# A decoder layer's row copies on two engines, homes of their own for window keys, and a compression weight loaded from ScalarE's queue

## What is computed

```python
kcmp = nsa_compress(full[:, :, 0], p['cmp_pe_k'], p['w_cmpk1'], p['w_cmpk2'])   # blocks of 64 rows -> one row
vcmp = nsa_compress(full[:, :, 1], p['cmp_pe_v'], p['w_cmpv1'], p['w_cmpv2'])   # gelu between the two weights
# o_c: attention over the compressed rows; their scores choose 16 blocks per query
# o_s: attention over the rows of the chosen blocks (k_sel, v_sel, from the cache pages)
# o_w: attention over a local window, the last 512 rows (k_win, v_win, from cache_win_kv)
o = g[..., 0:1] * o_c + g[..., 1:2] * o_s + g[..., 2:3] * o_w
```

## Time and profile before

| | us |
|---|---|
| median of 3 runs | 1168.5 |
| lowest, highest | 1167.29, 1168.63 |
| the profiled execution | 1166.26 |
| its span | 1164.6 |
| PE busy in the span | 1100.9 (95%) |
| DVE busy | 667.5 (57%) |
| ACT busy | 487.7 (42%) |
| POOL busy | 185.6 (16%) |
| DMA moved | 164.24 MB, mean 141 GB/s |

### The profile page before, as it was taken

The page is one execution under the profiler, slowest core; times in us unless marked ns, Lnnn a source line. Parts: engine busy times, 40 slices in busy tenths (PEclk is TensorE's granted clock), DMA queues, the critical chain, the costliest instruction groups (busy, mean ns, idle before and its releaser), DMA issues.

```text
span 1164.6 us, 22358 instructions
## 1 busy us (share of the span) xinstructions
PE 1100.9 (95%) x8538; PEld 1000.3 (86%) x8538; DVE 667.5 (57%) x1174; ACT 487.7 (42%) x773; POOL 185.6 (16%) x313
## 2 busy tenths in 40 slices
PE   6999999989599997999998989999999989999997
PEld 5888788778588785799988978899999989999997
DVE  4467993776476623566555576455533345666663
ACT  3200230357467523344334476463432234645541
POOL 1020023745123463000010030010000000001100
PEclk9999999999899998999999999999999999999999
DMA  6791253655538757476547435742542222232201
GB/s 203 172 247 54 83 186 116 175 137 129 135 86 262 230 145 226 144 214 198 189 112 258 130 107 169 262 137 84 171 138 80 79 99 78 73 109 73 73 1 77
DMA packets 172035, 164.24 MB, mean 141 GB/s; under 512 B 42341, under 2 KB 152962, under 8 KB 171802
## 3 DMA queue, kind: packets, MB, share of 16 engines
q1 hardware_dynamic: 161946, 134.77, 38.3%
q0 software_dynamic: 9984, 28.05, 8.2%
HBM read 154.21 MB, written 12.73 MB: 143 GB/s over the span
## 4 chain that ended last, share of the span: by engine, by line
PE 75%; SPq 7%; DVE 6%; issue 5%; ACT 4%; DMA 2%; POOL 0%; DVEq 0%; ACTq 0%
PE banks L1672 23%; PE banks L1926 15%; PE banks L1053 13%; PE banks L1319 3%; SPq L670 2%; PE banks L1623 2%; PE banks L1626 2%; SPq L690 2%; PE banks L1587 1%; PE banks L1059 1%; DVE rounded L3045 1%; PE banks L1386 1%; SPq L711 1%; SPq L721 1%; PE banks L1374 1%
## 5 line engine op out<-in xcount | busy, mean ns | idle before, releaser
L1672 PE MATMUL banks<-rounded 128*128 128x288 f32 (+1 forms) x2304 | 297.1, 289 | 3.1 <-DVE rounded L3172 2.6
L1672 PEld LDWEIGHTS banks<-rounded 128*128 128x128 f32 x2304 | 291.5, 188 | 6.7 <-DVE rounded L3172 3.3
L1926 PE MATMUL banks<-rounded 128*128 128x272 f32 x1536 | 195.1, 289 | 3.8 <-DVE rounded L3354 3.8
L1926 PEld LDWEIGHTS banks<-rounded 128*128 128x128 f32 x1536 | 194.5, 190 | 4.5 <-issue 3.1
L1053 PE MATMUL banks<-arena 128*128 128x256 f32 (+1 forms) x800 | 187.6, 394 | 0.0
L3045 DVE TENSOR_TENSOR rounded<-arena,rounded 128x2048 fp32r<-128x2048 f32 x63 | 146.1, 2319 | 71.0 <-ACT rounded L2156 70.9
L1053 PEld LDWEIGHTS banks<-arena 128*128 128x128 f32 x800 | 150.4, 190 | 31.8 <-issue 2.1
L2156 ACT ACTIVATE rounded<-arena 128x2048 fp32r<-128x2048 f32 x63 | 120.2, 1907 | 23.4 <-PE banks L1587 8.6
L3354 DVE TENSOR_TENSOR rounded<-arena,rounded 128x1088 fp32r<-128x1088 f32 x64 | 82.9, 1304 | 60.2 <-ACT rounded L2433 60.2
L2433 ACT ACTIVATE rounded<-arena 128x1088 fp32r<-128x1088 f32 x64 | 71.1, 1113 | 81.1 <-PE banks L1926 80.0
L2274 ACT ACTIVATE arena<-banks 128x256 f32<-128x256 f32 (+1 forms) x64 | 25.4, 397 | 126.5 <-PE banks L1672 126.5
(11 more groups left out here) (460 smaller groups left out, 1548.6 us busy)
## 6 DMA issues: line engine op xcount, KB each, us to landing
arena<-in_w_up SPq DMA_DIRECT2D x22, 1024.0 KB, 5.5
arena<-in_w_down SPq DMA_DIRECT2D x16, 1024.0 KB, 5.1
arena<-in_w_in SPq DMA_DIRECT2D x13, 1024.0 KB, 10.0
arena<-in_w_out SPq DMA_DIRECT2D x8, 1024.0 KB, 6.1
arena<-in_cache_mem_kv SPq DMA_DIRECT2D x16, 512.0 KB, 7.2
upper<-in_cache_nsa_kv SPq DMA_DIRECT2D x118, 64.0 KB, 2.2
upper<-in_cache_nsa_kv POOLq DMA_DIRECT2D x106, 64.0 KB, 2.4
arena<-in_cache_nsa_kv SPq DMA_DIRECT2D x90, 64.0 KB, 2.2
```

What stands on the lines that cost most here:

```text
L1672: ins = mm(bank(b, N), w[:, k], a[:, k, toks], start=(k == 0 and z == 0), stop=(k == K - 1 and z == 2))
L1926: ins = mm(bank(4 * (m % 2) + 2 * j + h, HALF), w[:, k, j * P:(j + 1) * P], h_split[:, t % 3, p, i, h * HALF:(h + 1) * HALF], start=(t % 1 ...
```

## The change

Four things are changed.

1. Window keys get four places of their own (`win_k`), in memory that is free after the prompt's attention. SP issues those of group 0 right after `prompt_attn_done`, those of group 1 between `sel_keys` and `sel_values`. `sel_keys` of group 1 runs in the order 0, 1, and kc 0 waits for `s_mm` 4, not 20. Window values of group 1 come last and wait for `sample_pv`; the memory rows wait for `s_mm` 40, where they waited for `snew_mm`.
2. Row copies of half 1, from tile 4 on, are shared: ACT copies tiles 4u and 4u + 2, DVE tiles 4u + 1 and 4u + 3, at pairs 8u and 8u + 1. A third semaphore, `relaid_2`, counts DVE's; `second_half_relaid` waits for both.
3. The four loads of `w2` move on SP from behind tile 7 to behind the first load of `w_cmpk1`.
4. `w_cmpv1` is loaded from ACT's queue: its first half behind the exps of pair 12, its second behind those of pair 16.

```diff
+        win_k = [place(512, at).rearrange("p (n d) -> p n d", n=WT)
+                 for at in (att0 + 4992, att0 + 5504, att0 + 1536, R + 25600)]
         def keys_page(b, kc):
-            return kv_pg[:, KV_AT[kc % 4], b, :, 0:P]
+            return win_k[b] if kc == 4 else kv_pg[:, KV_AT[kc], b, :, 0:P]
...
-                RELAY_AT.setdefault((1, 8 * _u + _k), []).append(4 * _u + _k)
+                RELAY_AT.setdefault((1 + _k % 2, 8 * _u + _k // 2), []).append(4 * _u + _k)
...
+        def second_half_relaid(eng, j):
+            if j < 4:
+                eng.wait_ge(sem("relaid_1"), j + 1)
+            else:
+                eng.wait_ge(sem("relaid_1"), 5 + (j - 4) // 2)
+                if j > 4:
+                    eng.wait_ge(sem("relaid_2"), (j - 3) // 2)
...
-            eng.wait_ge(sem("s_mm"), 20 if kc == 0 else KC_ORDER.index(kc) * 4 + 4)
+            eng.wait_ge(sem("s_mm"), KC_ORDER.index(kc) * 4 + 4)
...
                 if n == 3:
                     sp.wait_ge(sem("y_mm"), 8)
                     compress_weights(0, 0)
+                    for v, name in enumerate(("w_cmpk2", "w_cmpv2")):
+                        for h in range(2):
+                            sp.dma_start(w2[h * 64:h * 64 + 64, v, :], A[name][0]).then_inc(sem("w2_in"), 16)
...
-                if n == 7:
-                    for v, name in enumerate(("w_cmpk2", "w_cmpv2")):
...
-                if j in (9, 12):
-                    sp.wait_ge(sem("cmp_done"), 3 + (j == 12))
-                    compress_weights(1, int(j == 12))
...
+            window_keys(0)
+            window_values(0)
+            for kc in (0, 1):
+                sel_keys(sp, kc, known)
+            window_keys(1)
+            for kc in (0, 1):
+                sel_values(sp, kc, known)
             weights(1)
-            sp.wait_ge(sem("snew_mm"), NG2)
+            window_values(1)
+
+            weights(1)
+            sp.wait_ge(sem("s_mm"), NG2 * 20)
...
+                if i in (12, 16):
+                    part = int(i == 16)
+                    act.wait_ge(sem("cmp_done"), 3 + part)
+                    src = A["w_cmpv1"][0].rearrange("(s d) m -> s d m", d=HD)[:, part * 32:part * 32 + 32]
+                    for h in range(2):
+                        act.dma_start(w1[part][h * 64:h * 64 + 64, :, h * 64:h * 64 + 64], src).then_inc(sem(f"w1_in_{part}"), 16)
...
+                for j in RELAY_AT.get((2, i), ()):
+                    relay(dve, cp, j, 1, "relaid_2")
```

More of the change, by code:

```diff
@@ L671, in known_pages @@
                     for q in seqs for p in range(first, last)}
+        def second_half_relaid(eng, j):
[5 more added lines that the diff above has]
+                    eng.wait_ge(sem("relaid_2"), (j - 3) // 2)
         def raw_relaid(eng, j):
-            for half in range(2):
-                eng.wait_ge(sem(f"relaid_{half}"), j + 1)
+            eng.wait_ge(sem("relaid_0"), j + 1)
+            second_half_relaid(eng, j)
         def raw_pages(eng, j, known, first, last, arrived):
@@ L692, in raw_pages, with relay @@
                     .then_inc(sem(arrived), 16)
-        def relay(eng, copy, j, half):
+        def relay(eng, copy, j, half, name):
             u, k, slot = j // 4, j % 4, raw_slot(j)
@@ L701, in relay @@
             src = raw_rows(j).rearrange("p n (g d) -> p (n g) d", g=2)[:, :, half * 32:half * 32 + 32]
-            signal(copy(relaid[half][:, :, k * 32:k * 32 + 32], src.rearrange("p n d -> p d n")), f"relaid_{half}")
+            signal(copy(relaid[half][:, :, k * 32:k * 32 + 32], src.rearrange("p n d -> p d n")), name)
         def sel_keys(eng, kc, known):
@@ L830, in _, with window_keys, window_values @@
                     compress_weights(0, 1)
-                if n == 7:
-                    for v, name in enumerate(("w_cmpk2", "w_cmpv2")):
-                        for h in range(2):
-                            sp.dma_start(w2[h * 64:h * 64 + 64, v, :], A[name][0]).then_inc(sem("w2_in"), 16)
                 if j in (8, 9, 10):
                     known.update(known_pages(sp, (j - 3,), 0, SP_PAGES))
-                if j in (9, 12):
-                    sp.wait_ge(sem("cmp_done"), 3 + (j == 12))
-                    compress_weights(1, int(j == 12))
             win = A["cache_win_kv"][0]
[L843 to L856, removed]
+            def window_keys(gg):
                 for b in range(4):
                     w = win[gg * 4 + b].rearrange("(n p) z g d -> z p n (g d)", p=P)
-                    sp.wait_ge(sem("s_mm"), gg * 20 + b + 1)
-                    sp.dma_start(keys_page(b, 4), w[0]).then_inc(sem(f"k_win_{b}"), 16)
+                    if gg:
+                        sp.wait_ge(sem("s_mm"), 16 + b + 1)
+                    sp.dma_start(win_k[b], w[0]).then_inc(sem(f"k_win_{b}"), 16)
+            def window_values(gg):
+                if gg:
+                    sp.wait_ge(sem("sample_pv"), 4 * gg)
                 for b in range(4):
@@ L1312, in cmp1 @@
                         pe.wait_ge(*step(("w1a_zeroed", "w1b_zeroed")[part]))
-                        pe.wait_ge(sem(f"relaid_{part}"), 4 * u + 4)
+                        if part == 0:
+                            pe.wait_ge(sem("relaid_0"), 4 * u + 4)
+                        else:
+                            second_half_relaid(pe, 4 * u + 3)
                         if first:
@@ L2787, in _ @@
                 for half in range(2):
-                    relay(dve, cp, j, half)
+                    relay(dve, cp, j, half, f"relaid_{half}")
             for part, name in enumerate(("w1a_zeroed", "w1b_zeroed")):
```

11 lines of the change are left out of this document (8 added, 3 removed).

## The result

| | kernel before | changed kernel |
|---|---|---|
| median of the runs made together, us | 1167.89 (4 runs) | 1150.23 (4 runs, 1146.10 to 1150.52) |
| ratio | 1 | 0.9848, 95% interval 0.9823 to 0.9874 |
| profiled execution, us | 1166.26 | 1150.52 |
| its span, us | 1164.6 | 1148.8 |
| TensorE's wait ahead of the third compression, us | 11.64 | 1.84 |

The kernel is 17.7 us faster, 1.5%. The forecast was 13.9 us faster, 1154.6.

The account below looks back on a forecast made before the run. Two TensorE waits, 11.6 us before the third compression and 8.0 us for window keys, were taken as the bound. Window keys 10.6 + SP's queue 5.7 - clock 2.4 = 13.9 us off 1168.5 gives 1154.6, range 1150.3 to 1160.5.

Parts of the forecast that it names:

- Window keys: Second group of sequences: with early window keys its last steps take 3.9 us, not 14.5; gain 10.6 us.
- SP's queue: Ahead of the third compression: SP issues tile 11 earlier, TensorE resumes at 301.0; gain 5.7 us (3.5 to 7.1).
- the middle pace: Tile 10's nine page issues on SP: taken midway between 4.85 and 8.47 us, two issued before the weight.
- The clock: At the third compression: the clock still falls in a wait of about 6 us and takes back 2.4 us.
- 10.3 us after the fall: At the third compression: the lowered clock rises 10.3 us after falling, so TensorE loses 4.2 us against 1.8 before.
- The weight on ScalarE: Behind pairs 12 and 16: its issues cost nothing at half clock, 2.1 us if the clock holds.
- The rival in which the issues block ScalarE: Exps on ScalarE: four weight issues delay them, slower from 5.0 us each, 1172.3 us at 6; chance 0.03.
- Row copies: Prompt attention: six copies moved from ScalarE to VectorE cost zero, or 3.1 us if VectorE had no room.
- Carried through unchanged: Rest of the kernel behind the edited part: the gain stays whole, with no new TensorE wait past 500 us.
- pages at full pace: SP's pages beside the weight: not slowed, wait under 5 us, clock holds; gain 17.4 us, 1151.1 us; chance 0.08.
- DMA-bound pages: First wait: DMA engines limit the pages, so it keeps its length; gain 8.5 us, 1160.0 us; chance 0.10.
- unchanged second group: Second group: early window keys stand behind late pages and the wait stays; gain 3.3 us, 1165.2 us; chance 0.03.

Follow-up runs that it names:

- nine loads added: Changed kernel with nine more register loads on SP, of page numbers, between tiles 10 and 11; 1157.44 us.
- late loads: Changed kernel with two of SP's blocks of nine register loads moved from behind tiles 9 and 10 to behind tiles 11 and 12; 1145.91 us, again 1147.26.

## Why the prediction was off by 4.4 us

**Window keys: right, to 0.1 us.** Forecast 10.6 us; the stretch fell from 14.5 to 3.87 us. Removing the homes brought the wait back, adding them alone removed it.

**SP's queue: the mechanism right, the term mis-sized.** This is the step that failed most: pages of tile 10 at the middle pace, and tile 9 as before. (The sum has a slip as well: the middle of 299.6 and 303.2 is 301.4, a gain of 5.3 and a time of 1155.0, where it took 301.0 and 5.7. The "18 us of cover" of the window keys is 19.9 by its own figures; nothing hung on that.) I gave it 5.7 us with TensorE back at 301.0; it was 9.0 us with TensorE back at 297.77, outside my own 299.6 to 303.2. Tile 11's first page, forecast between 291.8 and 295.4, left at 289.24. By the rows:

- Tile 10's nine issues behind no weight: I took the middle of 4.85 and 8.47 us. They took 4.47, 4.0 us less than before. The middle was the wrong choice: it rested on how many of the nine issues come ahead of the weight (I said two; it was six), while the question was whether pages wait for a weight in another queue at all. They don't: with two ahead, as I had it, the nine take 4.76 us, back on SP they take 6.88, and with no weight at all the pages are no faster than with it on ScalarE. That explains 2.1 to 2.4 of the 4.0 us. The rest, 8.47 against 6.88 and 6.59 us behind a weight in the same queue, is gone even in edited kernels that leave the weight on SP, and no run shows why. The Trainium skill, "DMA: Bandwidth & Descriptors", section "Queues, rings and completion order", has the rule that SP and ScalarE have a ring each. The runs agree with it (4.76 against 6.88 us), and I gave its result 0.08. The Trainium skill says on the same page, section "Issuing engines are not separate DMA queues", that another engine saves the issue time alone. By that tile 10's nine would take as long beside the weight as behind it; here they do not (4.76 against 6.88 us).
- Tile 9's nine: 4.83 us where the kernel before had 6.30. It was not in the sum. All edited kernels whose rows show the nine apart have it, homes alone too, and no run shows why.
- Start of tile 9: 2.1 us earlier, forecast 1.2 for w2. With w2 moved it lies between 268.64 and 271.55 in ten profiles, with w2 at the old place between 270.53 and 272.01 in four. The move fits, but its size can't be read from these.
- Those three and the 2.3 us of the weight's own issue make 2.1 + 1.5 + 4.0 + 2.3 = 9.9, against 9.7 measured at tile 11. What the weight's move is shown to give is 4.8 of it (2.4 of issue and 2.4 of pages, from the kernel with the weight back on SP); the prediction had 4.1 for it (2.3 and 1.8). So the gain above the forecast is mostly what stays open. From there the data landed and were copied 0.8 us slower than before (7.3 us against 6.5), which leaves 9.0.

**The clock: forecast to take 2.4 us, took nothing.** The loss was 1.8 us before; after, it is 3.77 - 2.05 = 1.7. The failed step is "10.3 us after the fall". I read one length out of two waits and took it for fixed, and the wait that I applied it to, 6 us, became 1.84. The clock stays low for about 3.4 us in the changed kernel: the windows of 4 us show 0.85 and 0.72, the lower level is a half, so (0.15 + 0.28) / 0.5 x 4 us. In the same way the 4 us windows give 10.2 us in the kernel with nine loads added, behind 6.68 us, which is the case that I had forecast, but 6.8 us in the kernel with the weight back on SP, behind 7.12. The other step, that a wait under 5 us keeps the clock, fares no better: behind 1.84 us the clock fell, behind 3.02 and 3.68 us (no homes, w2 late) it did not, behind 4.22 it did. Which of the two comes can't be read from the length of such a wait.

**The weight on ScalarE: nothing, as in the sum, but for another reason.** I had it hidden by the slow clock, and 2.1 us visible without it. The rows of ScalarE and its queue:

```profile
302.03 0.60 ACTq L2122 DMA_DIRECT2D upper<-in_w_cmpv  x1
302.51 0.68 ACT L2115 ACTIVATE arena<-banks,arena 128x512 f32<-128x512 f32 x1
302.67 1.82 ACTq L2122 DMA_DIRECT2D upper<-in_w_cmpv  x1
...
303.18 0.69 ACT L2115 ACTIVATE arena<-banks,arena 128x512 f32<-128x512 f32 x1
...
304.61 1.99 ACT L2125 ACTIVATE upper<-upper 128x1024 f32<-128x1024 f32 x1 [0.66 <-issue]
```

The two issues last 0.60 + 1.82 = 2.4 us, but the exps run beside them, and only 0.66 us of idle time is left ahead of the row copy. I had added issue time to the engine's own; it overlaps. In the kernel without the weight TensorE's wait behind pair 16 is 0.22 us and with the weight on SP 0.23. With the weight on ScalarE it is 0.97 in the changed kernel, 0.52 and 0.99 in the two profiles with late loads, and between 0.41 and 0.99 in all: the issue costs TensorE 0.2 to 0.8 us, also at full clock. The rival in which the issues block ScalarE needed 5 us for each; the longest in any profile took 3.10 (2.33 in the changed kernel).

**Row copies: nothing on the whole, wrong in one place.** I wrote that the extra copies stand ahead of a maximum and cost nothing. One delays the probabilities of a pair, and TensorE's transposes wait 0.90 us for it at 275.50. In the changed kernel the later wait for SP's pages hides that. Where those pages come early it shows, as 0.7 us.

**Carried through unchanged: off by 3.4 us, within the spread of executions.** TensorE's chain of work behind the edited part (start, duration, line, count), the changed kernel first and then its repeat:

```profile
933.61 99.31 PE banks L1947 x768
```

```profile
934.42 96.69 PE banks L1947 x768
```

The same 768 matmuls took 98.14 us in the kernel before. In the changed kernel's window 900 to 940 us the granted clock was 0.91, in its repeat 1.00. That is 1.2 us more than before and 2.6 more than in its repeat. So 1.2 of the 3.4 us are a dip of the clock that was deeper in this one execution; 1.7 are the last 30 matmuls of the chain with 4.77 us against 3.10; 0.7 is the new wait at L1754, for the cached keys of the memory (in_cache_mem_kv). That is not the load of the memory rows (in_mem_prompt) which I had costed at nothing and at 1 us, and it stands in five of the twelve profiles of edited kernels only, so it is not shown to belong to the change (1.2 + 1.7 + 0.7 = 3.6; 0.2 came back in small steps). The first two change from one execution to the next (96.7 to 99.3 us and 3.1 to 5.7 us over all profiles), and so are nothing that the change does. They also set what one profiled execution can prove here: about 2 us. The kernel before spreads as much behind this point: from the start of group 1's gate matmuls to the end of the span are 696.3 and 701.1 us in its two profiles, and 695.4 to 700.2 in the twelve of edited kernels. In its second profile the granted clock is 0.50 from 692 to 700 us, and 1.00 in its first. So the 3.4 us are spread of executions as far as the runs show.

**The sum, with the sizes as measured:** 10.6 (window keys) + 9.0 (SP) + 0.1 (clock) - 0.5 (given back between there and the first group's gates, the wait behind pair 16 in it) = 19.2, and 19.2 - 3.4 = 15.8 us of span. Against the 13.9 of the forecast that is 1.9 more: SP +3.3, clock +2.5, pair 16 -0.5, the rest of the kernel -3.4. Another 1.9 us is that the median fell by 17.7 where the profiled executions differ by 15.7, and 0.6 that the kernel before had a lower median than in the forecast (1167.9, not 1168.5): 4.4 in all. No trace accounts for the 1.9 but the spread of executions, which for the kernel before went from 1163 to 1174 us over the batches.

Of the rivals, pages at full pace (1151.1) came nearest, though only its first half came true: the pages went at full pace and the wait fell below 5 us, but the clock fell. That it came within 0.9 us is luck: it had SP 1.9 us too low, the clock 1.7 too high, the wait behind pair 16 1.6 too dear, and nothing for the rest of the kernel, which took 3.4. DMA-bound pages and the unchanged second group are out by the rows above.

## What to carry to other kernels

When a queue is late, take its rows apart into three kinds, the transfers that the waiting engine needs, the transfers that only stand in front of them, and the register loads in between, and move the last two off it. Here a weight of two issues cost 2.4 us for itself and about 2 us for the nine pages behind it (6.6 to 6.9 us against 4.5 to 4.9), and nine register loads cost 5 us. Once the wait is down to what TensorE loses elsewhere anyway, expect little: in one of two profiles of the changed kernel TensorE came too late to have any use of SP's earliness, and taking the last 1.3 us off the wait gave 2.3 us, not clear of noise. Before giving a gain to an edit, undo the other parts too: homes alone, with no edit ahead of the first wait, shortened that wait from 11.64 to 7.67 us. A large transfer on another engine's queue did not slow the small ones; the same transfer in their queue did, so an idle engine's queue is worth more than the issue time that it saves.

## What the runs showed that I had not expected

- The granted clock did not follow the length of these short waits: it fell behind waits of 1.84 us and, once, 2.2 us after the end of a wait of 0.91 us, under a busy TensorE (not in the same kernel's other execution with 0.90 us), and held behind 3.02 and 3.68 us. Around the first wait it stayed at its lower level for 3.4 us (changed kernel), 6.8 us (weight on SP), 10.3 us (kernel before) and 13.7 us (kernel before, second profile).
- A DMA issue on ScalarE's queue overlaps the engine's running instructions: 2.4 us of issue, 0.66 us of idle time.
- Nine page issues of tiles 9 to 11 take 4.5 to 5.7 us with no weight ahead in their queue, but for tile 9 in the kernel before, and 6.6 to 8.5 us behind a weight in the same queue. Beside a weight in ScalarE's queue they took 4.5 to 4.9 in three profiles.
- The kernel before was slow at tile 9's nine issues (6.30 and 6.57 us) and at tile 10's (8.47 and 8.43 us) in both of its profiles. No edited kernel is, though one of them has the same code ahead of that point. This was not settled.
